# adaLN groups 3 to 5 on GpSimd instead of TensorE, in a two-layer diffusion backbone

## The chip, the cores and the metric

The kernel runs on one core of a Trainium2 chip. The metric is the device time of one execution in microseconds. TensorE multiplies matrices, VectorE (DVE in the profile) and ScalarE (ACT) do the elementwise work, GpSimd (POOL) takes some additions and a few transfers, and SyncE (SP) issues most of the loads.

## The reference, cut to what matters

The network has two layers over 512 latent and 256 context tokens of width 1024. Each layer is modulated by a vector `mod` of 6 x 1024 numbers, which comes from a product of the condition with `w_ada`, once for the latent tokens (`c`) and once for the context tokens (`c_ctx`):

```python
for l in range(DEPTH):
    mod   = silu_c  @ w_ada[l] + b_ada[l]        # w_ada: (2, 1024, 6144)
    mod_c = silu_cc @ w_ada[l] + b_ada[l]
    sh1, sc1, gt1, sh2, sc2, gt2 = jnp.split(mod, 6, axis=-1)
    h = modulate(rmsnorm(x, g_mix[l]), sh1, sc1)
    ...                                          # w_in, attention and convolution
    x = x + gt1 * merge_groups(...)
    h2 = modulate(rmsnorm(x, g_ffn[l]), sh2, sc2)
    x = x + gt2 * swiglu(h2, w_gate_up[l], w_down[l])
    ...                                          # the same for ctx, in layer 0 only
```

The result is the latent stream after a last RMSNorm. `mod` of layer 1 is needed only once layer 0 is over, so its product can be done at any time before.

## The kernel before, in words

Features lie on the partitions, 128 at a time, and tokens in the free dimension (768 in layer 0, 512 in layer 1). Each layer goes through phases in a fixed order, `PHASES`: `u`, `qkv`, attention, `ob`, `oa`, and then the feed-forward part in three chunks of 8, 8 and 6 tiles: `gu0`, `dn0`, `gu1`, `dn1`, `gu2`, `dn2`. A phase is a row of blocks of weights, two (a pair, `j` = 0 and 1) for each `i`: `gu0` and `gu1` have 16 blocks, `gu2` 12, each `dn` phase 8. One block of layer 0 is `tile_product` (L457): for each of 8 k-tiles (6 in `dn2`) three products (high x high, low x high, high x low) over two column ranges, so 48 (36) matmuls. `after` lets another piece of work be issued behind a certain k of a block.

The weights are split on the chip: SP loads `raw`, ScalarE copies it to `w_high` (`split_high`, L677), VectorE subtracts (`split_low`, L945, `w_low`). In a `gu` phase VectorE reads a product out of PSUM (`scale_product`, L989), then does `split_low` for the next pair, after the second product multiplies gate and value (L1283), and forms `ff_low` (L1287) once ScalarE has made `ff_high`. The next `dn` phase waits for one `ff_low` tile at each k of its first block (`ready`).

The adaLN product is cut into 6 groups, three for each layer, of 2048 columns, and each group into 8 units, one for each 128 rows of `w_ada`. A unit is a tile of 128 x 2048 numbers (1 MB). `ada_unit` (L406) multiplies it on TensorE with the 32 columns of `cond` (of which two are used), in four products of 512 columns that lie side by side in the array and add up in PSUM over the 8 units. Then ScalarE copies the sum (`ada_rows`), TensorE turns it (`ada_turn`) and VectorE adds the bias and forms the gains (`ada_columns`). Group 0 runs at the start, groups 1 and 2 in `u` and `qkv` of layer 0, and groups 3, 4 and 5, which are layer 1's, in `dn0`, `dn1` and `dn2` of layer 0: one unit after each block. Their tiles are loaded by SP between the loads of `raw`, into two places in turn. A phase with units is written out; the others are loops over `i`.

GpSimd has nothing to do from the end of `oa` of layer 0 up to layer 1's convolution. Each engine runs its own stream in order; semaphores tie them together. `Chain.link` makes an instruction of an engine wait for the one before it.

Of the kernel before, what the change touches and what calls it, by code (L numbers as in the profile page):

```python
# [27 lines left out]
P = 128  # L28
D = 1024
DT = D // P  # L30
# [23 lines left out]
AG = 3  # L54
# [70 lines left out]
def hybrid_backbone(nc, xT, params, w_ada, w_conv, w_mix, w_out, w_gu, w_dn0, w_dn1, w_dn2,  # L125
                    rope, ident_in, masks_in, out):
    with ExitStack() as ctx:
# [13 lines left out]
        ada_in_qkv = wD[:].rearrange("p j g m -> p (j g m)")  # L141
        ssum = sb("ssum", [P, T])
# [3 lines left out]
        ada_row = act_out[:, 0:AGW // 4]  # L146
# [4 lines left out]
        diag = scratch[:].rearrange("p (b t) -> p b t", t=P)  # L151
        par = sb("par", [P, COLS])
# [9 lines left out]
        ones = sb("ones", [P, P])  # L162
        per_tok = sb("per_tok", [P, 2, TB])
# [9 lines left out]
        with ExitStack() as h_scope:  # L173
# [22 lines left out]
            with ExitStack() as s:  # L196
                s.enter_context(nc.sbuf_tensor("gap_ff", [P, 2 * max(CHUNKS) * T], F32))
                ada_in_ff = s.enter_context(nc.sbuf_tensor("ada_in_ff", [P, AGW], F32))
            with ExitStack() as s:
# [26 lines left out]
        ada_in = [sem(f"ada_in{j}") for j in range(2)]  # L226
        first_in = [sem(f"ada_first_in{j}") for j in range(DT)]
# [7 lines left out]
        ada_mm, ada_rowed = sem("ada_unit_done"), sem("ada_rows_copied")  # L235
        ada_tr, ada_cols = sem("ada_rows_transposed"), sem("ada_columns_ready")
# [82 lines left out]
        def ada_units(layer, name, block):  # L319
# [4 lines left out]
            at = (0, 1, 1, 2, 3, 3, 4, 5) if name == "qkv" else [k * (blocks - 1) // (DT - 1) for k in range(DT)]  # L324
# [3 lines left out]
        ADA_PLACES, uses, last_use = {}, [0, 0], [DT, DT]  # L328
        for g in range(1, 2 * AG):
            for k in range(DT):  # L330
# [4 lines left out]
                ADA_PLACES[g, k] = (tile, ada_in[place], 16 * uses[place], last_use[place])  # L335
                last_use[place] = g * DT + k + 1
        for k in range(DT):
            ADA_PLACES[0, k] = (ada_first[k][:] if k < DT - 1 else ada_raw[:], first_in[k], 16, 0)
# [8 lines left out]
        def _(sp):  # L347
            sp.dma_start(par[:], params).then_inc(par_in, 16)

            def load_ada(unit):  # L350
                tile, landed, _, free = ADA_PLACES[unit]
                if free:
                    sp.wait_ge(ada_mm, free)
# [49 lines left out]
        def _(pe):  # L403
# [11 lines left out]

            def ada_turn(g):

                pe.wait_ge(ada_rowed, g + 1)
                for j in range(4):
                    last = nc.tensor.transpose(bank[:, SMALL, P * j:P * j + P], ada_row[:, P * j:P * j + P], ident[:])  # L420
# [78 lines left out]
            def phase(layer, name, ktiles, rhsH, rhsL, cols, ready=None, key=None, blocks=TB):  # L499
# [3 lines left out]
                after = {0: [], 1: []}  # L503
                if key is not None:
# [997 lines left out]
```

## Time and profile before

| | us |
|---|---|
| median of three runs | 1657.31 (1656.78 to 1658.14) |
| the profiled execution | 1658.43 |
| its span | 1656.1 |
| TensorE busy | 1570.3 (95%) |
| VectorE busy | 837.1 (51%) |
| ScalarE busy | 570.1 (34%) |
| GpSimd busy | 126.3 (8%) |

The span is the time from the first to the last instruction of the profiled execution. In the views, PE is TensorE's matmuls and PEld its weight loads. L465 is the product in `tile_product`, L412 the one in `ada_unit`, L420 the turn in `ada_turn`. A line like "x<-x,tmp" names the tile written and the tiles read.

### The profile page before, as it was taken

Reading aid. Unit: us, or ns where it says so; the run is one execution under the profiler, and the core shown is the slowest. Engines: PE = TensorE matmul, PEld = TensorE weight load, DVE = VectorE, ACT = ScalarE, POOL = GpSimd, SP = SyncE. Lnnn points to the kernel's source line nnn. Section 1 sums busy time; section 2 is a strip of 40 time slices with the busy share of each in tenths; the row PEclk is TensorE's granted clock in tenths of the full one; section 3 lists DMA queues with packets and bytes.
Section 4 is the critical chain, followed back from the end, with each engine's and each line's share of the span. In section 5 each row is a group of like instructions: output and inputs, shape, how many; then the busy total and the mean of one; then the engine's idle time right before and its main releaser. Section 6 shows DMA issues by size and latency. Waiting matters only on the chain.

```text
span 1656.1 us, 25043 instructions
## 1 busy us (share of the span) xinstructions
PE 1570.3 (95%) x9804; PEld 1278.1 (77%) x9804; DVE 837.1 (51%) x1527; ACT 570.1 (34%) x882; POOL 126.3 (8%) x162
## 2 busy tenths in 40 slices
PE   3899987999999999999999999988999999999997
PEld 0675654578888878888788878765578998998995
DVE  1484566867433322433233455767776443443445
ACT  2411258734443111221122233136845541321222
POOL 0032012021000000000000000521120000000000
PEclk9999988999999999999999999998999999999998
DMA  8474420002112442124412353511012223323222
GB/s 325 178 219 107 177 91 1 1 26 65 56 59 63 165 153 64 63 63 139 171 60 63 104 199 104 144 52 39 1 39 90 89 90 100 89 89 100 91 76 88
DMA packets 39865, 161.19 MB, mean 97 GB/s; under 512 B 5616, under 2 KB 6000, under 8 KB 33648
## 3 DMA queue, kind: packets, MB, share of 16 engines
q1 hardware_dynamic: 35856, 148.72, 26.7%
q0 software_dynamic: 3936, 11.45, 2.6%
q8 instruction: 51, 0.84, 0.2%
q14 instruction: 22, 0.18, 0.0%
HBM read 149.76 MB, written 2.10 MB: 92 GB/s over the span
## 4 chain that ended last, share of the span: by engine, by line
PE 84%; DVE 7%; ACT 4%; issue 2%; DMA 2%; SPq 1%; POOL 0%; DVEq 0%; ACTq 0%; POOLq 0%
PE banks L465 71%; PE banks L494 3%; PE banks L572 2%; PE banks L584 2%; PE banks L599 2%; PE banks L412 2%; DMA x<-in_xT 1%; PE banks L452 1%; PE banks L435 1%; DVE w_low L949 1%; ACT prob L765 1%; DVE ssum L956 1%; DMA raw<-in_w_mix 0%; ACT w_high L684 0%; DVE row_max L1048 0%
## 5 line engine op out<-in xcount | busy, mean ns | idle before, releaser
L465 PE MATMUL banks<-h_high,w_high 128*128 128x512 f32 (+1 forms) x1856 | 433.3, 315 | 5.0 <-DVE h_low L978 3.5
L465 PE MATMUL banks<-h_high,w_low 128*128 128x512 f32 (+1 forms) x1856 | 428.8, 313 | 0.0
L465 PE MATMUL banks<-h_low,w_high 128*128 128x512 f32 (+1 forms) x1856 | 428.6, 312 | 0.0
L684 ACT ACTIVATE w_high<-raw 128x1024 fp32r<-128x1024 f32 (+1 forms) x178 | 185.5, 1042 | 672.8 <-PE banks L465 664.5
L949 DVE TENSOR_TENSOR w_low<-raw,w_high 128x1024 fp32r<-128x1024 f32 (+1 forms) x178 | 217.6, 1222 | 238.7 <-ACT w_high L684 236.6
L465 PEld LDWEIGHTS banks<-h_high,w_high 128*128 128x128 f32 x1856 | 289.0, 190 | 40.1 <-issue 18.8
L465 PEld LDWEIGHTS banks<-h_low,w_high 128*128 128x128 f32 x1856 | 288.4, 190 | 21.6
L465 PEld LDWEIGHTS banks<-h_high,w_low 128*128 128x128 f32 x1856 | 287.3, 190 | 21.6
L992 DVE COPY shift_product<-banks 128x2 f32<-128x2 f32 x116 | 18.4, 159 | 354.0 <-PE banks L465 342.2
L465 PE MATMUL banks<-ff_high,w_high 128*128 128x512 f32 (+1 forms) x528 | 162.5, 362 | 0.5 <-DVE ff_low L1287 0.5
L465 PE MATMUL banks<-ff_low,w_high 128*128 128x512 f32 (+1 forms) x528 | 160.0, 357 | 0.0
L465 PE MATMUL banks<-ff_high,w_low 128*128 128x512 f32 (+1 forms) x528 | 160.0, 357 | 0.0
L465 PEld LDWEIGHTS banks<-ff_high,w_high 128*128 128x128 f32 x528 | 86.8, 188 | 33.3 <-issue 17.6
L465 PEld LDWEIGHTS banks<-ff_low,w_high 128*128 128x128 f32 x528 | 87.0, 188 | 15.9
L465 PEld LDWEIGHTS banks<-ff_high,w_low 128*128 128x128 f32 x528 | 86.9, 188 | 16.0
L993 DVE TENSOR_TENSOR tmp<-banks,inv_root 128x768 f32<-128x768 f32 (+1 forms) x116 | 95.1, 820 | 0.1
L572 PE MATMUL banks<-k_stacked,q_stacked 128*128 128x384 f32 (+2 forms) x224 | 63.3, 389 | 12.9 <-ACT esink L767 8.0
L1048 DVE TENSOR_REDUCE row_max<-banks 128x1 f32<-128x512 f32 (+2 forms) x80 | 55.2, 690 | 32.8 <-PE banks L572 32.6
L901 ACT ACTIVATE ff_high<-tmp 128x768 f32 (+3 forms) x44 | 32.5, 740 | 97.9 <-DVE tmp L1283 97.9
L1024 DVE SCALAR_TENSOR_TENSOR x<-banks,mod,x 128x512 f32 (+1 forms) x96 | 60.3, 656 | 11.1 <-PE banks L465 11.0
L1287 DVE TENSOR_TENSOR ff_low<-tmp,ff_high 128x768 f32 (+3 forms) x44 | 36.3, 826 | 43.7 <-ACT ff_high L901 43.7
L777 ACT ACTIVATE probT<-banks 128x512 f32<-128x512 f32 (+2 forms) x80 | 48.0, 600 | 29.2 <-PE banks L584 28.7
(147 smaller groups left out, 1582.9 us busy)
## 6 DMA issues: line engine op xcount, KB each, us to landing
raw<-in_w_gu SPq DMA_DIRECT2D x88, 512.0 KB, 3.5
ada_raw<-in_w_ada SPq DMA_DIRECT2D x21, 1024.0 KB, 5.1
raw<-in_w_dn SPq DMA_DIRECT2D x32, 512.0 KB, 3.6
raw<-in_w_mix SPq DMA_DIRECT2D x28, 512.0 KB, 5.5
ada_in_ff<-in_w_ada SPq DMA_DIRECT2D x12, 1024.0 KB, 5.0
raw<-in_w_out SPq DMA_DIRECT2D x16, 512.0 KB, 3.6
ada_first<-in_w_ada SPq DMA_DIRECT2D x7, 1024.0 KB, 13.5
raw<-in_w_dn SPq DMA_DIRECT2D x16, 384.0 KB, 3.0
```

The lines of the kernel that those rows point to most:

```text
L412: last = mm(bank[32 * q:32 * q + 32, ADA, :], cond[:, k, :], tile[:, 512 * q:512 * q + 512], start=(k == 0), stop=(k == DT - 1), tile_posi ...
L465: last = mm(bank[:, 2 * slot + bk, 0:b - a], weights[w][:, k0_w + k, :], rhs[:, k0_rhs + k, a:b], start=(k == 0 and n == 0), stop=(k == kt ...
L494: last = mm(bank[QC * q:QC * q + QC, BC + bk, 0:b - a], wD[:, j, g, QC * q:QC * q + QC], zr[j][:, q, SH * g + a:SH * g + b], start=(g == 0 ...
L572: last = mm(wide[:, at:at + w], lhs, rhs, start=in_bank[m] not in in_bank[:m], stop=in_bank[m] not in in_bank[m + 1:], skip_group_check=True)
L584: last = nc.tensor.transpose(wide[:, 512 * PTB + P * m:512 * PTB + P * m + P], probs[u % 4][:, P * m:P * m + P], ident[:])
L684: f(wH[j][:, 0:k, :], raw[j][:, 0:k, :], ACT.Copy).then_inc(w_high, 1)
L777: f(PT[:, group % 2, 0:w, i % 2 * 2 + i // 2, :], wide[:, 512 * PTB:512 * PTB + P * w].rearrange("p (k q) -> p k q", k=w), ACT.Copy).then_ ...
L949: tt(wL[j][:, 0:k, :], raw[j][:, 0:k, :], f32(wH[j][:, 0:k, :]), ALU.subtract).then_inc(w_low, 1)
L993: tt(like(tmp[slot]), src, like(rs), ALU.mult).then_inc(slot_free[slot], 1)
L1024: last = stt(out=xt, in0=bank[:, 2 * slot + (a >= N), 0:b - a], scalar=mod[:, layer, bass.ds(t + gate * DT, 1), v], in1=xt, op0=ALU.mult, ...
L1048: nc.vector.reduce_max(mx[:, c:c + 1], score_place(u, qs[q][2]), AX.X).then_inc(row_ok, 1)
L1287: tt(aL[:, i, 0:width], tmp[1][:, 0:width], f32(aH[:, i, 0:width]), ALU.subtract).then_inc(ff_low, 1)
```

## The change

Groups 3 to 5 leave `ada_unit`. GpSimd loads their 24 tiles itself, from two places in turn, as soon as its own work in `oa` of layer 0 is done. For each tile and for each of the two conditions (v = 0, 1) it multiplies with the column of `cond` of that tile, each partition by its own number, and adds the product to a running sum `ada_sums[v]` of 128 x 2048, in two halves of 1024 columns. The running sums lie in `w_conv` and where `ssum`, `sq` and `tmp` begin to be laid out in a scope of their own. After the eighth tile of a group TensorE adds the partitions once (`ada_sum`): `pick` has a column of ones at place v, so eight products give the two rows. `ada_sum` and the turn stand in the second block of `gu1` for group 3, in the second block of `gu2` for group 4 and in the last block of `gu2` for group 5, behind k = 1 and k = 6. The first tile of a group waits until TensorE has read the group before. `gu1`, `gu2` and the `dn` phases of layer 0 change their form with it: the `dn` phases become loops, and the last pair of `gu2` is written out.

```diff
+        ada_sums = [ada_in_qkv, ada_sum_ctx[:]]
+        ada_row = [act_out[:, 0:AGW // 4]] * 3 + [scratch[:, 0:AGW // 4]] * 3
...
-        ADA_IN = {(0, "u"): 1, (0, "qkv"): 2, (0, "dn0"): 3, (0, "dn1"): 4, (0, "dn2"): 5}
-
-        TURN_IN = {(0, "qkv"): 1, (0, "gu1"): 3, (0, "gu2"): 4, (1, "u"): 5}
+        ADA_IN = {(0, "u"): 1, (0, "qkv"): 2}
+        SUM_IN, TURN_IN = {(0, "gu1"): 3, (0, "gu2"): 4}, {(0, "qkv"): 1}
+        LAST_SUM = (0, "gu2")
...
+            def ada_sum(g):
+
+                pe.wait_ge(ada_read, DT * (g - 2))
+                for v in range(2):
+                    for q in range(4):
+                        last = mm(bank[32 * q:32 * q + 32, ADA, :], pick[:, v, :], ada_sums[v][:, 512 * q:512 * q + 512],
+                                  start=(v == 0), stop=(v == 1), tile_position=(0, 32 * q))
+                last.then_inc(ada_mm, 1)
...
+                if (layer, name) in SUM_IN:
+                    g = SUM_IN[layer, name]
+                    after[1].append((1, lambda: ada_sum(g)))
+                    after[1].append((DT - 2, lambda: ada_turn(g)))
...
                 if loop:
-                    with pe.Fori(1, pairs) as i:
+                    with_sum = (layer, name) == LAST_SUM
+                    with pe.Fori(1, pairs - with_sum) as i:
                         for j in range(2):
                             gemm_block(layer, name, i, j, ktiles, rhsH, rhsL, cols)
+                    if with_sum:
+                        for j in range(2):
+                            gemm_block(layer, name, pairs - 1, j, ktiles, rhsH, rhsL, cols,
+                                       after=[(1, lambda: ada_sum(5)), (DT - 2, lambda: ada_turn(5))] if j else ())
...
+                if layer == 0:
+                    later = [(g, k) for g in range(3, 2 * AG) for k in range(DT)]
+
+                    def load_ada(unit):
+                        tile, landed, _, free = ADA_PLACES[unit]
+                        pool.wait_ge(*free)
+                        pool.dma_start(tile, w_ada[unit[0], unit[1]]).then_inc(landed, 16)
+
+                    pool.wait_ge(gemm, 2 * USES[layer, "gu0"])
+                    for unit in later[0:2]:
+                        load_ada(unit)
+                    pool.wait_ge(diag_ok, root_index[layer, "n2"] + 1)
+                    for at, unit in enumerate(later):
+                        tile, landed, count, _ = ADA_PLACES[unit]
+                        pool.wait_ge(landed, count)
+                        if unit[1] == 0:
+                            pool.wait_ge(ada_mm, 3 * DT + unit[0] - 3)
+                        for h in range(2):
+                            half = slice(h * AGW // 2, (h + 1) * AGW // 2)
+                            for v in range(2):
+                                c = cond[:, unit[1], v:v + 1]
+                                if unit[1] == 0:
+                                    last = nc.gpsimd.tensor_scalar(ada_sums[v][:, half], tile[:, half], c, None, ALU.mult)
+                                else:
+                                    chain.link(nc.gpsimd.tensor_scalar(ada_part[:], tile[:, half], c, None, ALU.mult))
+                                    last = nc.gpsimd.tensor_tensor(ada_sums[v][:, half], ada_sums[v][:, half], ada_part[:],
+                                                                   ALU.add)
+                                if h + v < 2:
+                                    chain.link(last)
+                        last.then_inc(ada_read, 1)
+                        pool.wait_ge(ada_read, at + 1)
+                        if at + 2 < len(later):
+                            load_ada(later[at + 2])
```

Left out of the diff: ScalarE's and VectorE's `ada_rows` and `ada_columns` move with the sums (the first and last tile of `gu1` and `gu2`), and the waits are renumbered.

## Rows read from the trace of the kernel before

**Rows 1.** The page: its first line, and the chain that ended last by engine.
```profile
span 1656.1 us, 25043 instructions
...
PE 84%; DVE 7%; ACT 4%; issue 2%; DMA 2%; SPq 1%; POOL 0%; DVEq 0%; ACTq 0%; POOLq 0%
```

**Rows 2.** Chain in order of time, `dn0` to `dn2`: start us, us, what.
```profile
560.60 1.00 PE banks L412 x8
...
627.94 0.99 PE banks L412 x8
...
845.97 0.44 PE banks L420 x4
846.40 103.49 PE banks L465 x588
949.89 0.99 PE banks L412 x8
...
994.93 1.00 PE banks L412 x8
```

**Rows 3.** GpSimd's groups, shapes apart: xcount | busy us, mean ns | idle before.
```profile
L1382 POOL TENSOR_TENSOR ssum<-ssum,conv 128x768 f32<-128x768 f32 x1 | 1.8, 1849 | 0.1
...
L1341 POOL DMA_DIRECT2D w_conv<-in_w_conv x6 | 3.5, 592 | 0.3 <-issue 0.3
...
L1382 POOL TENSOR_TENSOR ssum<-ssum,conv 128x512 f32<-128x512 f32 x1 | 1.3, 1291 | 0.1
...
L1335 POOL MEMSET cond<- 128x256 f32 x1 | 0.3, 312 | 0.3 <-POOLq L1494 0.3
L1337 POOL MEMSET ones<- 128x128 f32 x1 | 0.2, 205 | 0.0
```

**Rows 4.** GpSimd in order of time: start us, us, engine, line, operation.
```profile
153.79 1.86 POOL L1380 TENSOR_TENSOR ssum<-conv 128x768 f32<-128x768 f32 x1
155.72 1.85 POOL L1382 TENSOR_TENSOR ssum<-ssum,conv 128x768 f32<-128x768 f32 x1
...
353.39 2.80 POOL L1409 TENSOR_TENSOR x<-x,tmp 128x768 f32<-128x768 f32 x1 [1.51 <-DVE tmp L1035]
```

**Rows 5.** VectorE in order of time, beside those GpSimd instructions.
```profile
244.75 0.15 DVE L1061 TENSOR_TENSOR psums<-psums,esink 128x1 f32<-128x1 f32 x1
...
246.90 1.80 DVE L1061 TENSOR_TENSOR psums<-psums,esink 128x1 f32<-128x1 f32 x1
...
353.26 1.23 DVE L949 TENSOR_TENSOR w_low<-raw,w_high 128x1024 fp32r<-128x1024 f32 x1
```

**Rows 6.** GpSimd in order of time, layer 0's attention.
```profile
244.88 7.59 POOL L1404 TENSOR_TENSOR z_padded<-z_padded,inv_root 128x768 f32<-128x768 f32 x4 [32.90 <-ACT inv_root L705]
```

**Rows 7.** VectorE's groups in 841 to 944 us (`gu2` of layer 0), shapes apart.
```profile
L949 DVE TENSOR_TENSOR w_low<-raw,w_high 128x1024 fp32r<-128x1024 f32 x11 | 13.5, 1226 | 8.5 <-ACT w_high L684 8.2
...
L1287 DVE TENSOR_TENSOR ff_low<-tmp,ff_high 128x768 f32 x5 | 4.8, 959 | 5.7 <-ACT ff_high L901 5.7
L1283 DVE SCALAR_TENSOR_TENSOR tmp<-tmp,shift_product,act_out 128x512 f32<-128x512 f32 x5 | 3.7, 746 | 0.0
L1283 DVE SCALAR_TENSOR_TENSOR tmp<-tmp,shift_product,act_out 128x256 f32<-128x256 f32 x5 | 2.4, 480 | 0.0
```

**Rows 8.** VectorE in order of time, the `n2` diagonals of layer 0.
```profile
422.49 1.27 DVE L971 TENSOR_SCALAR diagonals<-ident,per_tok 128x128 f32<-128x128 f32 x6
```

**Rows 9.** Chain in order of time, the first blocks of the kernel.
```profile
52.54 11.04 PE banks L465 x48
...
64.58 8.65 PE banks L465 x48
```

**Rows 10.** TensorE in order of time, the first products of `dn0`.
```profile
551.96 0.51 PE L465 MATMUL banks<-ff_high,w_high 128*128 128x512 f32 x2
```

**Rows 11.** VectorE in order of time, the last tile of `gu0`.
```profile
552.16 0.16 DVE L992 COPY shift_product<-banks 128x2 f32<-128x2 f32 x1 [6.12 <-PE banks L465]
...
556.46 0.96 DVE L1287 TENSOR_TENSOR ff_low<-tmp,ff_high 128x768 fp32r<-128x768 f32 x1 [0.91 <-ACT ff_high L901]
```

**Rows 12.** TensorE's waits over the whole kernel: us in total, times, longest.
```profile
PE banks L465 <- DVE ff_low L1287: 0.5, 1, 0.5
```

More of the change, by code:

```diff
@@ L226, in hybrid_backbone @@
         ada_in = [sem(f"ada_in{j}") for j in range(2)]
+        ada_late_in = [sem(f"ada_late_in{j}") for j in range(2)]
         first_in = [sem(f"ada_first_in{j}") for j in range(DT)]
@@ L323, in ada_units @@
             blocks = 2 * PAIRS_OF[name]
-            at = (0, 1, 1, 2, 3, 3, 4, 5) if name == "qkv" else [k * (blocks - 1) // (DT - 1) for k in range(DT)]
+            at = (0, 1, 1, 2, 3, 3, 4, 5) if name == "qkv" else [blocks // DT * k for k in range(DT)]
             return [(ADA_IN[layer, name], k) for k in range(DT) if at[k] == block]
-        ADA_PLACES, uses, last_use = {}, [0, 0], [DT, DT]
+        ADA_PLACES, uses, last_use = {}, [0, 0], [(ada_mm, DT), (ada_mm, DT)]
         for g in range(1, 2 * AG):
@@ L352, in load_ada @@
                 if free:
-                    sp.wait_ge(ada_mm, free)
+                    sp.wait_ge(*free)
                 if unit == (ADA_IN[0, "qkv"], 1):
@@ L513, in phase @@
                                    after[j] if i == 0 else ())
-                        for u in ada_units(layer, name, 2 * i + j):
-                            ada_unit(u)
+                        if with_ada:
+                            for u in ada_units(layer, name, 2 * i + j):
+                                ada_unit(u)
                         if (name, 2 * i + j) in CONV_AFTER:
@@ L627, in attention @@
                     values(len(qs) - 1, m)
-            pe.wait_ge(consts, 4)
+            pe.wait_ge(consts, 5)
             pe.wait_ge(cond_ok, 1)
@@ L891, in _, with gu_pair @@
                     ff = layer * FT + sum(CHUNKS[:c])
-                    def gu_pair(i):
+                    def gu_pair(i, first=False, last=False):
                         split_high(layer, gu, i, 0)
@@ L896, in gu_pair @@
                         for a, b, v in streams(context):
-                            last = f(act_out[:, a:b], tmp[0][:, a:b], ACT.Silu, bias=shifted[:, 0, v:v + 1])
-                        last.then_inc(gate_ok, 1)
+                            gate = f(act_out[:, a:b], tmp[0][:, a:b], ACT.Silu, bias=shifted[:, 0, v:v + 1])
+                        gate.then_inc(gate_ok, 1)
+                        if last and (layer, gu) == LAST_SUM:
+                            ada_rows(5)
+                        if first and (layer, gu) in SUM_IN:
+                            ada_rows(SUM_IN[layer, gu])
                         split_high(layer, gu, i, 1)
@@ L901, in gu_pair @@
                         f(aH[:, i, 0:width], tmp[1][:, 0:width], ACT.Copy).then_inc(ff_high, 1)
-                    with act.Fori(0, tiles - 1) as i:
+                    gu_pair(0, first=True)
+                    with act.Fori(1, tiles - 1) as i:
                         gu_pair(i)
-                    gu_pair(tiles - 1)
+                    gu_pair(tiles - 1, last=True)
                     def dn_pair(i, more=True):
@@ L1189, in _ @@
                         taps(10 * i - 5, 10 * i + (i == 3))
-                    if layer and i == 0:
-                        ada_columns(ADA_IN[0, "dn2"])
                 for i in range(3):
@@ L1288, in gu_pair @@
                         dve.wait_ge(ff_low, i + (ff + 1))
-                    with dve.Fori(0, tiles - 1) as i:
+                    gu_pair(0)
+                    if (layer, gu) in SUM_IN:
+                        ada_columns(SUM_IN[layer, gu])
+                    with dve.Fori(1, tiles - 1) as i:
                         gu_pair(i)
                     gu_pair(tiles - 1)
+                    if (layer, gu) == LAST_SUM:
+                        ada_columns(5)
                     def dn_pair(i, more=True):
@@ L1337, in _ @@
             nc.gpsimd.memset(ones[:], 1.0).then_inc(consts, 1)
+            nc.gpsimd.memset(pick[:], 0.0).then_inc(consts, 1)
+            pool.wait_ge(consts, 4)
+            for v in range(2):
+                nc.gpsimd.memset(pick[:, v, v:v + 1], 1.0)
             nc.gpsimd.memset(mean_col[:, 0:1], 1.0 / D)
@@ L1369, in _ @@
                 if layer:
-                    pool.wait_ge(ada_mm, DT * (ADA_IN[0, "qkv"] + 1))
+                    pool.wait_ge(ada_mm, 3 * DT + 3)
                 for k in (1, 2):
```

28 lines of the change are left out of this document (17 added, 11 removed).

## The prediction

> **What bounds the kernel now.** I read the page first. The profiled execution took 1658.43 us, with a span of 1656.1 us; the median of the three timed runs is 1657.31. 84% of the chain that ended last is TensorE [rows 1]. So whatever leaves TensorE's stream in layer 0 comes off the time, and whatever makes TensorE wait is added. Then I read the chain in order of time through the feed-forward part of layer 0. The reader is to see there that the adaLN units stand on the chain itself, one behind each block of `dn0`, `dn1` and `dn2` [rows 2]. All changes below are made against the profiled execution and carried over to the median.
>
> **What is removed.** The chain has 103.49 us for 588 products, which is 12.25 blocks of 48, so 8.45 us for a block with nothing between its products [rows 2]. In `dn0` the units stand at 560.60 and, seven later, at 627.94: a period of 9.62 us, so one unit costs 1.17 us (0.99 of its own and some 0.2 where TensorE changes over). In `dn2` a block has 36 products, 6.34 us at the same rate; the period is (994.93 - 949.89) / 6 = 7.51 us, again 1.17 [rows 2]. 24 units leave: 24 x 1.17 = **28.1 us off**. Their 24 loads leave SP's queue for GpSimd's. SP has no wait for them on the chain, so that is worth nothing.
>
> **What is added to TensorE.** `ada_sum` issues eight such products, two rounds of the four that make a unit: 2 x 0.99 + 0.2 = 2.2 us, three times: **6.6 us on**. The three turns are as many as before at 0.44 us each [rows 2] and only move. ScalarE copies the rows of the sum while TensorE does k = 2 to 6 of the same block, 5 x 1.06 = 5.3 us, so the turn finds them ready. The new columns work on VectorE is a few instructions of 16 columns. The unrolled `dn` phases become loops like `gu2`, whose blocks are those of 8.45 us, so the form costs nothing. Balance so far: -28.1 + 6.6 = -21.5 us.
>
> **What GpSimd has to do for one group.** The sums of a group take, for k = 0, four one-input instructions of 128 x 1024, and for k = 1 to 7 four pairs of one multiplication and one addition: 32 multiplications and 28 additions, each waiting for the one before by `chain.link`.
> - Addition (two inputs): 1849 ns for 768 columns and 1291 ns for 512 [rows 3], so 2.18 ns a column and 2407 ns for 1024. From one linked instruction to the next is 155.72 - 153.79 = 1.93 us against 1.86 us of the instruction [rows 4], so 0.07 us more each. 28 x 2.48 = 69.4 us.
> - Multiplication by a column (one input): no row shows one on GpSimd. From below it is bounded by the memset, which reads nothing: 312 ns for 256 columns, 205 ns for 128 [rows 3], 0.84 ns a column, so 0.95 us for 1024. From above by the addition, which reads twice: 2.41 us. I take 1.2 us, near the memset, since one stream of input is missing there and the addition's second stream is missing too. 32 x 1.27 = 40.6 us.
> - Issue of the loads: 6 fall inside the time of the last group, and 592 ns is what such an issue takes for half the size [rows 3]: 6 x 0.59 = 3.5 us, at most 7.
> So W = 113 us for a group if nobody is in the way; 152 with the upper bound, 105 with the lower.
>
> On the multiplication the Trainium skill speaks too (GPSIMD Engine Reference, "Engine selection"): a one-input operation on GpSimd runs at roughly line rate, a two-input one at about half VectorE's speed. By that the multiplication would be some 1.0 us, an estimate from that page, and the sum below some 6 us smaller. No trace here shows it.
>
> **GpSimd and VectorE get in each other's way.** An addition of GpSimd that began at 353.39 took 2.80 us instead of 1.85; VectorE's `w_low`, with two SBUF inputs, had begun at 353.26 and ran its usual 1.23 us [rows 4, 5]. The other way round, while GpSimd does four additions in a row from 244.88 [rows 6], an addition of one column on VectorE that should take 0.15 us takes 1.80 us and ends with the GpSimd instruction [rows 5]. So the two exclude each other for the length of an instruction, in order of arrival.
> VectorE's instructions with two SBUF inputs in a stretch of ten `gu2` blocks: 10 `w_low` at 1.23, 5 pairs of L1283 at 0.75 + 0.48, 5 of L1287 at 0.96 [rows 7]: 23.3 us. In the one case where I can see it, 0.95 of 1.23 us came on top of GpSimd's instruction, so I count D = 21 us; its bounds are 0 (they slip between) and 23.
>
> **Where the groups must be done.** Group 3 starts when the `n2` diagonals are made, at 422.49 + 1.3 = 423.8 [rows 8], and is wanted in the second block of `gu1`. That is some 210 us later: `gu0` and `dn0` are 24 blocks. Even 152 + 33 (VectorE in `gu0`) + 12 fits. Group 4 starts when the sum of 3 is read and is wanted 24 blocks later, 203 us: it fits also. Group 5 can't start before TensorE has read group 4 in `gu2`'s second block, since the running sums are the same two tiles, and it is wanted in `gu2`'s twelfth block after k = 1. Between them lie k = 2 to 7 of block 1, nine blocks, and k = 0 and 1 of block 11: ten blocks and a turn, 84.5 + 0.4 = **84.9 us**. GpSimd needs W + D = 113 + 21 = 134 us. TensorE stands at `pe.wait_ge(ada_read, 24)` for 134 - 85 = **49 us**; behind that wait are the rest of the block and all of `dn2`, so nothing hides it. Bounds: 105 - 85 = 20 us; 152 + 23 + 3 - 85 = 93 us.
> After such a rest TensorE starts slowly: the first 48 products after its early wait took 11.04 us against 8.65 for the next [rows 9]: **2.4 us**.
>
> **The two turns from `gu` to `dn`.** The first block of `dn0` wants `ff_low` of the last tile at its k = 7, 551.96 + 7.4 = 559.4 [rows 10]. VectorE begins the tail at 552.16 and ends `ff_low` at 557.42 [rows 11]: 1.9 us to spare. The tail has four instructions that can meet GpSimd. `w_low` comes at a random moment (about 1 us of wait), the two of L1283 come right behind another, with a GpSimd instruction let in between (half 2.48, half 1.27: 1.9 us each), and `ff_low` comes 0.9 us later (about 0.9): 5.5 us, so 3.6 us late. GpSimd is still at work then in `gu0` (95 of its 113 us are done by 552) and `gu1`: 2 x 3.6 = **7 us**; bounds 0 and 2 x (4 x 2.48 - 1.9) = 16. At `gu2` the whole group is done before `dn2` starts; the 0.5 us that TensorE waits for `ff_low` in the whole kernel stay [rows 12]. In the middle of a phase the same delays are hidden: a pair's `w_low` is wanted 8.45 us or more after its product is read.
>
> **The sum.** -28.1 + 6.6 + 49 + 2.4 + 7 = +36.9 us. Profiled execution 1658.4 + 37 = 1695, median 1657.3 + 37 = **1694 us**.
>
> **The rivals.**
> 1. *The multiplication costs as much as the addition.* W = 152, the wait 152 + 21 - 85 = 88 us: 1657.3 - 21.5 + 88 + 2.4 + 7 = 1733. For it: GpSimd's two-input rate is itself far from one column a cycle, so its programs may be slow whatever they read. Against: the memset row. 17%.
> 2. *GpSimd and VectorE hardly meet.* D = 0 and no late `ff_low`: wait 28 us, 1657.3 - 21.5 + 28 + 2.4 = 1666. For it: only short overlaps are seen. Against: both directions are in the trace. 12%.
> 3. *Faster: at 1024 columns GpSimd works at the memset's rate in the additions too*, 0.95 us each. Place: group 5 in `gu2`. Then W = 60 x 1.02 + 3.5 = 65 us and 65 + 19 fits into 85; nothing is left but the balance: 1657.3 - 21.5 = 1636. It decides from W + D under 85 + 12 = 97 us, 12 us for a unit; there the wait is smaller than what is saved net of the late `ff_low` and the slow start. Against: the slope of 2.18 ns a column between 512 and 768. 8%.
> Between rivals 2 and 3 lies a narrow case of no difference: 3%.
>
> **How the numbers follow.** Forecast 60% (own range 1680 to 1712: the multiplication at 0.95 to 1.5 us, the late `ff_low` at 0 to 11 us), rival 1 17%, rival 2 12%, rival 3 8%, no difference 3%. The range is to leave out rival 3 and the case of no difference and takes in the bounds of the wait, 20 to 93 us: 1657.3 - 21.5 + 20 + 2.4 = 1658 to 1657.3 - 21.5 + 93 + 2.4 + 11 = 1742; I put the low end at 1661. About 0.2%, 3.3 us, is what a measurement of this kernel tells from no change. Faster 0.08, same 0.04, slower 0.88.
>
> **What would show it.** In the changed kernel's profile: `dn` blocks of layer 0 at 8.45 and 6.34 us without units; GpSimd multiplications of 128 x 1024 near 1.2 us and additions near 2.4, some longer by a VectorE instruction; groups 3 and 4 done before they are wanted; one long TensorE wait for GpSimd in the last block of `gu2`, some 49 us, with ScalarE and VectorE idle in it; short waits for `ff_low` early in `dn0` and `dn1`. The prediction is wrong if a unit takes GpSimd less than 12 us, if the wait stands elsewhere (at `gu1` or `gu2`'s start), or if TensorE waits for `w_low` within the phases.

## The result, and the profile after

The changed kernel takes 1727.26 us (median of four runs, 1725.49 to 1728.79) against 1657.72 us for the kernel before beside it: a ratio of 1.042, 95% interval 1.0402 to 1.0438. It is slower by 69.5 us. The forecast was 1694 us within 1661 to 1742; the measured time lies inside these bounds, near their upper end, and outside the forecast's own narrower range of 1680 to 1712.

First the changed kernel's page: the span, the busy time of the engines, the chain that ended last by engine and the start of its list by line.

```profile
span 1724.2 us, 24982 instructions
...
PE 1548.5 (90%) x9660; PEld 1275.2 (74%) x9660; DVE 910.3 (53%) x1527; ACT 535.9 (31%) x856; POOL 646.2 (37%) x369
...
PE 75%; POOL 10%; DVE 7%; ACT 4%; issue 2%; DMA 1%; SPq 1%; DVEq 0%; ACTq 0%; POOLq 0%
```

TensorE did less work (1548.5 us busy, 1570.3 before) and the kernel is longer all the same; GpSimd, which had no share of the chain [rows 1], has 10% of it. TensorE's waits over the whole kernel say where (us in total, times, longest):

```profile
PE banks L434 <- POOL ada_sum_context L1476: 91.2, 1, 91.2
...
PE banks L487 <- DVE w_low L985: 0.7, 1, 0.7
PE banks L487 <- DVE ff_low L1321: 0.5, 1, 0.5
```

In the changed kernel's rows L434 is the product in `ada_sum`, L487 the one in `tile_product` and L442 the turn. The new loss is one wait, at `ada_sum(5)`. The waits for `w_low` and `ff_low` stay under 1 us each; the one for `ff_low` is as long as before [rows 12]. The chain in order of time shows the rest of the layer (start us, us, what). These lines answer to [rows 2].

```profile
424.60 204.03 PE banks L487 x1158
628.63 1.85 PE banks L434 x16
630.48 5.46 PE banks L487 x30
635.95 0.44 PE banks L442 x4
636.38 197.73 PE banks L487 x1122
834.12 1.90 PE banks L434 x16
836.06 0.13 issue
836.19 2.85 POOL w_conv L1473
...
1009.87 2.35 POOL ada_sum_context L1476
1012.26 3.64 PE banks L434 x16
1015.90 6.48 PE banks L487 x30
1022.38 0.44 PE banks L442 x4
1022.82 51.95 PE banks L487 x294
```

The reader sees `gu0` and `dn0` in one unbroken piece of products (1158 in 204.03 us, so 8.46 us for 48), a sum of 1.85 us where eight units were, and the same for `gu1` and `dn1`. From 836.19 us the chain is GpSimd's, until the third sum at 1012.26. The forecast named this place. What it missed is why the piece is so long. GpSimd's groups, shapes apart, in 420 to 1100 us (xcount | busy us, mean ns | idle before); they answer to [rows 3]:

```profile
L1475 POOL TENSOR_SCALAR ada_part<-ada_in_ff,cond 128x1024 f32<-128x1024 f32 x48 | 151.2, 3151 | 4.1
L1475 POOL TENSOR_SCALAR ada_part<-ada_raw,cond 128x1024 f32<-128x1024 f32 x36 | 111.1, 3087 | 3.1
L1476 POOL TENSOR_TENSOR ada_sum_context<-ada_sum_context,ada_part 128x1024 f32<-128x1024 f32 x42 | 106.1, 2525 | 3.5
L1476 POOL TENSOR_TENSOR w_conv<-w_conv,ada_part 128x1024 f32<-128x1024 f32 x42 | 102.7, 2444 | 3.5
```

The multiplication, which reads one tile, takes longer than the addition, which reads two. In the chain, where TensorE waits and VectorE is idle, a unit is quite regular (start us, us, what):

```profile
946.86 2.86 POOL ada_part L1475
949.79 2.35 POOL w_conv L1476
952.14 0.09 issue
952.22 2.85 POOL ada_part L1475
...
968.26 0.51 issue
968.76 0.60 POOL ada_in_ff L1457
969.41 2.86 POOL ada_part L1475
```

A pair of a multiplication and an addition takes 952.22 - 946.86 = 5.36 us, a unit (all that GpSimd does with one tile) 969.41 - 946.86 = 22.55 us: four pairs and 1.1 us for its last semaphore and the issue of the next load.

After the wait TensorE is slow for a moment. The columns are the stretch, its length, the busy us of PE, PEld, DVE, ACT and POOL, the granted clock, the DMA share and GB/s; the granted clock goes from 1.00 (2.4 GHz) down to 0.53 in the wait (nearly all of it at 1.2 GHz), and is 0.75 in the mean just after:

```profile
836.00:921.00 85.00, 85.00 (x484) 74.21 (x484) 47.73 (x48) 20.50 (x26) 80.84 (x31) 1.00 0.28 95
921.00:1012.00 91.00, 0.07 (x1) 0.00 (x0) 0.00 (x0) 0.18 (x1) 86.59 (x36) 0.53 0.11 39
1012.00:1024.00 12.00, 11.74 (x58) 7.78 (x59) 0.08 (x1) 0.68 (x2) 0.21 (x1) 0.75 0.01 1
```

The third sum took 3.64 us instead of 1.85, and the 30 products behind it 6.48 instead of 5.46: 2.8 us in all.

The sum of what is seen: 23 units at 1.17 us off (-26.9; why 23 and not 24 is told below), three sums at 1.87 (+5.6), the wait (+91.2), the slow start (+2.8): +72.7 us. The chain can be measured over the same stretch in both kernels, from the start of the first long piece of products to the last product of `dn2`. In the kernel before this stretch began and ended so:

```profile
426.50 134.09 PE banks L465 x762
...
995.92 6.57 PE banks L465 x36
```

It took 1002.49 - 426.50 = 575.99 us, and in the changed kernel 1074.77 - 424.60 = 650.17: +74.2 us. Beyond the 72.7 that is the third turn (0.44 us), which stood in layer 1 before, and 1.1 us spread over the products. The spans differ by 68.1 us only: 1.9 us were gained before the stretch (424.60 instead of 426.50) and 4.2 behind it. Of the latter, 1.6 us are in the first pieces of layer 1, where the granted clock was 0.73 before (1009.3 to 1022 us) and 0.86 after (1081.6 to 1094 us), and 0.4 the turn; the rest isn't traced. The kernel before itself varies from 1651.4 to 1658.3 us over the runs below, so differences of this size outside the stretch aren't put down to the change.

### The profile page after: what moved, and what is told of

It is laid out like the page before. It is cut to its first block, busy times and chain, and to the rows that moved or that the text cites. A ratio compares the mean times of both kernels' runs of the same rounds, so it can differ in the third digit from the quotient of the medians.

```text
span 1724.2 us, 24982 instructions
## 1 busy us (share of the span) xinstructions
PE 1548.5 (90%) x9660; PEld 1275.2 (74%) x9660; DVE 910.3 (53%) x1527; ACT 535.9 (31%) x856; POOL 646.2 (37%) x369
## 3 DMA queue, kind: packets, MB, share of 16 engines
q1 hardware_dynamic: 32400, 123.56, 21.5%
## 4 chain that ended last, share of the span: by engine, by line
PE 75%; POOL 10%; DVE 7%; ACT 4%; issue 2%; DMA 1%; SPq 1%; DVEq 0%; ACTq 0%; POOLq 0%
PE banks L487 63%; POOL ada_part L1475 5%; PE banks L516 3%; PE banks L604 2%; PE banks L616 2%; POOL ada_sum_context L1476 2%; POOL w_conv L1476 2%; PE banks L631 2%; DMA x<-in_xT 1%; PE banks L474 1%; PE banks L457 1%; DVE w_low L985 1%; ACT prob L797 1%; PE banks L425 1%; DVE ssum L992 0%
## 5 line engine op out<-in xcount | busy, mean ns | idle before, releaser
L487 PE MATMUL banks<-h_high,w_high 128*128 128x512 f32 (+1 forms) x1856 | 433.8, 315 | 4.1 <-DVE h_low L1014 3.5
L487 PE MATMUL banks<-h_high,w_low 128*128 128x512 f32 (+1 forms) x1856 | 429.2, 313 | 0.0
L487 PE MATMUL banks<-h_low,w_high 128*128 128x512 f32 (+1 forms) x1856 | 428.7, 312 | 0.0
L985 DVE TENSOR_TENSOR w_low<-raw,w_high 128x1024 fp32r<-128x1024 f32 (+1 forms) x178 | 249.3, 1401 | 181.1 <-ACT w_high L716 178.8
L487 PEld LDWEIGHTS banks<-h_high,w_high 128*128 128x128 f32 x1856 | 289.5, 190 | 39.8 <-issue 18.4
L487 PEld LDWEIGHTS banks<-h_low,w_high 128*128 128x128 f32 x1856 | 288.7, 190 | 21.6
L487 PEld LDWEIGHTS banks<-h_high,w_low 128*128 128x128 f32 x1856 | 287.3, 190 | 21.6
L487 PE MATMUL banks<-ff_high,w_high 128*128 128x512 f32 (+1 forms) x528 | 160.5, 358 | 0.5 <-DVE ff_low L1321 0.5
L487 PE MATMUL banks<-ff_high,w_low 128*128 128x512 f32 (+1 forms) x528 | 160.5, 358 | 0.0
L487 PE MATMUL banks<-ff_low,w_high 128*128 128x512 f32 (+1 forms) x528 | 160.4, 358 | 0.0
L1475 POOL TENSOR_SCALAR ada_part<-ada_in_ff,cond 128x1024 f32<-128x1024 f32 x48 | 151.2, 3151 | 4.1
L1475 POOL TENSOR_SCALAR ada_part<-ada_raw,cond 128x1024 f32<-128x1024 f32 x36 | 111.1, 3087 | 3.1
L1476 POOL TENSOR_TENSOR ada_sum_context<-ada_sum_context,ada_part 128x1024 f32<-128x1024 f32 x42 | 106.1, 2525 | 3.5
L1476 POOL TENSOR_TENSOR w_conv<-w_conv,ada_part 128x1024 f32<-128x1024 f32 x42 | 102.7, 2444 | 3.5
L487 PEld LDWEIGHTS banks<-ff_high,w_high 128*128 128x128 f32 x528 | 87.1, 188 | 17.0 <-DVE ff_low L1321 0.9
L487 PEld LDWEIGHTS banks<-ff_high,w_low 128*128 128x128 f32 x528 | 87.1, 188 | 16.1
L487 PEld LDWEIGHTS banks<-ff_low,w_high 128*128 128x128 f32 x528 | 87.1, 188 | 16.0
L1398 POOL DMA_DIRECT2D z_shifted<-z_padded x96 | 46.9, 497 | 128.4 <-issue 81.3
L434 PE MATMUL banks<-w_conv,pick_stream 128*32 128x512 f32 x24 | 4.1, 757 | 91.2 <-POOL ada_sum_context L1476 91.2
```

The source lines that it names most:

```text
L487: last = mm(bank[:, 2 * slot + bk, 0:b - a], weights[w][:, k0_w + k, :], rhs[:, k0_rhs + k, a:b], start=(k == 0 and n == 0), stop=(k == kt ...
L985: tt(wL[j][:, 0:k, :], raw[j][:, 0:k, :], f32(wH[j][:, 0:k, :]), ALU.subtract).then_inc(w_low, 1)
L1398: pool.dma_start(zr[k % 2][QC * c:QC * c + QC, q, 0:w], z[QC * q:QC * q + QC, k, c:c + w])\
L1475: chain.link(nc.gpsimd.tensor_scalar(ada_part[:], tile[:, half], c, None, ALU.mult))
L1476: last = nc.gpsimd.tensor_tensor(ada_sums[v][:, half], ada_sums[v][:, half], ada_part[:], ALU.add)
```

## The experiments

**Only the first tile of each group has arithmetic.** This separates the wait from everything else that the change does. All 24 tiles are still loaded.

```diff
+                        if unit[1] == 0:
...
-                                    chain.link(nc.gpsimd.tensor_scalar(ada_part[:], tile[:, half], c, None, ALU.mult))
-                                    last = nc.gpsimd.tensor_tensor(ada_sums[v][:, half], ada_sums[v][:, half], ada_part[:],
-                                                                   ALU.add)
...
+                        else:
+                            last = nc.gpsimd.tensor_copy(ada_part[:, 0:1], tile[:, 0:1])
```

> The changed kernel, but GpSimd does its arithmetic for the first tile of each group only (the other seven tiles are loaded and not added, so layer 1's modulation is left incomplete). Theory A: the added time is TensorE's single wait of 91.2 us for group 5 and the slow start behind it (about 2.9 us); everything else of the change is a gain. Then this is 1727.3 - 91.2 - 2.9 = 1633 us, no wait of TensorE for GpSimd, and w_low back at 1.23 us. Worked out from the edit, 23 units at 1.17 off and three sums at 1.9 on give 1657.7 - 26.9 + 5.6 = 1636. Theory B (GpSimd's work costs TensorE time in the phases too, by making VectorE late): clearly below 1633, say 1625.

Measured: 1634.60 us (1634.27 to 1635.99) against 1655.13 for the kernel before; ratio 0.9876 (0.9853 to 0.9899). TensorE waits nowhere for GpSimd's sums, so their loads alone delay nothing. Theory A said 1633; B's 1625 isn't met. Better than the total is the chain: `gu0` and `dn0` took the same time with idle GpSimd as in the changed kernel, where GpSimd was at work all the while (there 204.03 and 197.73 us as well).

```profile
424.69 204.03 PE banks L487 x1158
...
636.48 197.73 PE banks L487 x1122
```

So GpSimd's work beside VectorE, as the changed kernel has it, costs TensorE nothing in these phases, to a hundredth of a microsecond. The gain of taking the units away, 20.5 us here in the medians and 19.8 in the chain from the first long piece to the last product of `dn2` (556.18 us against 575.99), is close to the 21.5 of the forecast's balance.

**Additions only.** Without the multiplications of tiles 1 to 7, the time of a group is tested term by term.

```diff
-                                    chain.link(nc.gpsimd.tensor_scalar(ada_part[:], tile[:, half], c, None, ALU.mult))
-                                    last = nc.gpsimd.tensor_tensor(ada_sums[v][:, half], ada_sums[v][:, half], ada_part[:],
+                                    last = nc.gpsimd.tensor_tensor(ada_sums[v][:, half], ada_sums[v][:, half], tile[:, half],
```

> The changed kernel without the multiplications of tiles 1 to 7: GpSimd adds the tile itself to both running sums (the factor is left out of the computation). Theory A (a group's time is the sum of its instructions, and the multiplication at 2.93 us from start to start was the term that was too small): a group takes 7 x 11.1 + 12.8 - 1 = 89 us and 7 to 12 us for VectorE's turns, so TensorE waits 11 to 16 us for group 5: about 1633 + 14 + 2 = 1649, about equal to or a little faster than the kernel before. Theory B (VectorE's two-input instructions are shut out and counted in full, 21 us): the wait is 25 us, 1660. Theory C (something other than the arithmetic delays group 5, such as the loads): the wait stays above 60 us.

Measured: 1651.63 us (1650.45 to 1654.19); ratio 0.9977 (0.9966 to 0.9988), just faster than the kernel before. TensorE's wait for group 5 (its waits over the whole kernel):

```profile
PE banks L434 <- POOL ada_sum_context L1475: 12.8, 1, 12.8
```

12.8 us lie inside Theory A's 11 to 16, not at the 25 of B or above the 60 of C (the loads). The multiplications are worth 91.2 - 12.8 = 78.4 us of the wait: 28 x 2.93 = 82 less some of VectorE's turns, which now all fall on additions.

**Multiplication by a fixed number.** Is it the column of the condition that makes it slow?

```diff
-                                    chain.link(nc.gpsimd.tensor_scalar(ada_part[:], tile[:, half], c, None, ALU.mult))
+                                    chain.link(nc.gpsimd.tensor_scalar(ada_part[:], tile[:, half], 0.5, None, ALU.mult))
```

> The changed kernel with the multiplication of tiles 1 to 7 by the number 0.5 instead of a column with one number for each partition (the condition is left out there). If the column makes the multiplication slow, it falls from 2.85 us to 1.0 to 1.5 us, group 5 takes some 40 us less and TensorE's wait falls from 91 to about 50 us: 1685. If it is the operation's own rate, it stays at 2.85 us and the time at 1727.

Measured: 1727.39 us in one run, the wait 88.0 us. The multiplication took nearly as long with VectorE at work beside it (3007 and 3053 ns in the mean, 3151 and 3087 in the changed kernel), and 2.77 instead of 2.85 us while VectorE is idle:

```profile
953.11 2.77 POOL L1475 TENSOR_SCALAR ada_part<-ada_in_ff 128x1024 f32<-128x1024 f32 x1
```

The column is worth 0.08 us of the 2.85; it is not the cause. The time didn't fall with the wait because TensorE waited 2.3 us in three pieces for `ff_low` here, where it waited 0.5 in the changed kernel.

**The multiplication as a two-input instruction.** The same result, with the column read again for each element.

```diff
-                                    chain.link(nc.gpsimd.tensor_scalar(ada_part[:], tile[:, half], c, None, ALU.mult))
+                                    chain.link(nc.gpsimd.tensor_tensor(ada_part[:], tile[:, half],
+                                                                       c.to_broadcast([P, AGW // 2]), ALU.mult))
```

> The changed kernel, same result, but the multiplication is a two-input instruction: tile times the condition's column read again for each of the 1024 columns (step zero). If GpSimd's cost goes with the kind of instruction, the multiplication falls from 2.85 us to the addition's 2.40, a group takes 28 x 0.45 = 13 us less, and TensorE's wait is 91 - 13 = 78 us, a few more if VectorE is shut out longer: about 1716. If it goes with the arithmetic (multiplying by a column), 2.85 stays and the time is 1727.

Measured: 1712.67 us in one run, the wait 67.9 us, more saved than I expected. GpSimd in order of time, while TensorE waits:

```profile
945.25 1.90 POOL L1475 TENSOR_TENSOR ada_part<-ada_in_ff,cond 128x1024 f32<-128x1024 f32 x1
947.23 2.34 POOL L1477 TENSOR_TENSOR w_conv<-w_conv,ada_part 128x1024 f32<-128x1024 f32 x1
```

The two-input form takes 1.90 us, below the addition and a third below the one-input form. So the same multiplication costs less as a two-input instruction than as a one-input one, the opposite order of the one that I had assumed. Why it is also cheaper than the addition (2.34 us) no run isolates. Multiplying as such isn't the reason: with two full inputs, four multiplications of 768 columns took 7.59 us in the kernel before [rows 6], 1.9 us each, like the additions of that size [rows 3]. What is left is the second input, one column read with a step of zero. The two-input form has a price of its own: TensorE now waits 7.0 us, in three pieces of up to 3.4, for `ff_low`:

```profile
PE banks L487 <- DVE ff_low L1321: 7.0, 3, 3.4
```

The two long pieces of products, with the turns from `gu` to `dn` in them, take 208.85 and 202.94 us instead of 204.03 and 197.73, 10.0 us more together. That is why the time falls by 14.6 us and not by the 23.3 us of the wait. This is the late `ff_low` that the forecast had expected for the changed kernel.

**One-input instructions only.** How long does each kind keep VectorE out?

```diff
-                                    last = nc.gpsimd.tensor_tensor(ada_sums[v][:, half], ada_sums[v][:, half], ada_part[:],
-                                                                   ALU.add)
+                                    last = nc.gpsimd.tensor_scalar(ada_sums[v][:, half], ada_part[:], c, None, ALU.mult)
```

> The changed kernel with each addition replaced by a second multiplication of one input (so the sum over the tiles is left out; the running sums hold only the last tile). Theory A: a one-input instruction of GpSimd keeps VectorE's two-input instructions out only for a part of its 2.85 us (some 0.9 us, while it reads), a two-input one for its whole 2.4 us. Then w_low in gu0 to dn1 falls from a mean of 1.76 us to 1.2 to 1.45 and ff_low from 2.1 to under 1.4, although GpSimd is busier. Theory B: any GpSimd instruction keeps VectorE out for its full length: w_low at 1.8 us or more. In both the group takes 28 x 0.45 = 13 us more, so the wait is about 100 us and the time 1737.

Measured: 1739.65 us in one run, the wait 101.7 us, as expected in both theories. GpSimd and then VectorE in order of time, one stretch of `gu0`:

```profile
450.88 2.85 POOL L1476 TENSOR_SCALAR w_conv<-ada_part,cond 128x1024 f32<-128x1024 f32 x1
...
466.85 2.85 POOL L1475 TENSOR_SCALAR ada_part<-ada_raw,cond 128x1024 f32<-128x1024 f32 x1
```

```profile
451.13 1.95 DVE L985 TENSOR_TENSOR w_low<-raw,w_high 128x1024 fp32r<-128x1024 f32 x1
...
468.02 1.22 DVE L985 TENSOR_TENSOR w_low<-raw,w_high 128x1024 fp32r<-128x1024 f32 x1
469.17 1.14 DVE L1317 SCALAR_TENSOR_TENSOR tmp<-tmp,shift_product,act_out 128x512 f32<-128x512 f32 x2
```

A `w_low` that comes 1.17 us after a multiplication's start (468.02 against 466.85) runs at its usual 1.22 us, inside it. One that comes 0.25 us after a start (451.13 against 450.88) takes 1.95 us, so it began in earnest some 1.0 us after that start. In the changed kernel a `ff_low` meets an addition:

```profile
864.91 2.40 POOL w_conv L1476
```

```profile
865.16 2.96 DVE L1321 TENSOR_TENSOR ff_low<-tmp,ff_high 128x768 f32 x1 [1.14 <-ACT ff_high L937]
```

It ends at 868.12, 0.81 us after the addition's end at 867.31. Its usual time is 0.96 us, so it ran only when the addition was all but over. The means over `gu0` to `dn1`, in ns, from VectorE's groups of each kernel:

| | before | changed | additions only | one input only |
|---|---|---|---|---|
| `w_low`, 1024 columns | 1226 | 1762 | 1582 | 1316 |
| L1283 / L1317, 512 columns | 746 | 1516 | 2138 | 1058 |
| L1283 / L1317, 256 columns | 480 | 661 | 1545 | 584 |
| `ff_low` (the larger group) | 959 | 2145 | 1936 | 1261 |

The columns aren't equally full of GpSimd's work: it was busy 349 of these 412 us in the changed kernel and 188 with additions only, where it had its groups done early, so that column is diluted. With one input only the means fall into the bounds of Theory A (1.2 to 1.45 us for `w_low`, under 1.4 for `ff_low`). Theory A holds: the one-input multiplication keeps VectorE's two-input instructions out for about its first microsecond only, the addition to its end. The Trainium skill ("SBUF — State Buffer", section "SBUF: two separate sides") says that whichever of the two starts first holds the shared port pair for the whole instruction. For GpSimd's additions the trace agrees (the 2.96 us above); for its multiplications it doesn't (1.0 of 2.85 us).

**Pieces of 512 columns.** What of each instruction goes with the columns?

```diff
-                        for h in range(2):
-                            half = slice(h * AGW // 2, (h + 1) * AGW // 2)
+                        for h in range(4):
+                            half = slice(h * AGW // 4, (h + 1) * AGW // 4)
...
```

> The changed kernel with every multiplication and addition in two pieces of 512 columns, same result: it gives what of each instruction goes with the columns. The addition should take 1.29 us, as the 512-column addition of the kernel before. The multiplication: 1.5 us if its 2.85 us are all per column, 2.0 us or more if a large part is fixed. With 1.5 the group takes 60 x 0.25 = 15 us more and the time is 1742; with 2.0 it takes 32 us more, 1760.

Measured: 1763.20 us in one run. GpSimd in order of time, while TensorE waits:

```profile
962.59 1.56 POOL L1475 TENSOR_SCALAR ada_part<-ada_raw,cond 128x512 f32<-128x512 f32 x1
964.24 1.26 POOL L1476 TENSOR_TENSOR ada_sum_context<-ada_sum_context,ada_part 128x512 f32<-128x512 f32 x1
```

The multiplication goes from 2.85 to 1.56 us, so 2.5 ns a column and 0.27 us fixed; the addition from 2.35 to 1.26, 2.1 ns a column and 0.17 fixed. Most of the multiplication is a rate, as the lower of my two cases had it. The time is above that case's 1742 all the same, so the time was forecast wrong. The two multiplications and two additions that now stand for a pair take 2 x 3.01 = 6.02 us instead of 5.36; the 0.66 us, where I had reckoned with 0.5, make the wait for group 5 20 us longer (111.4). Groups 3 and 4 were late too: TensorE waited three times, 118.9 us in all. These are 27.7 of the 35.9 us by which this run is above the changed kernel. Another 2.6 are in the first two sums (2.70 and 3.69 us instead of 1.85 and 1.90, each behind a wait); the rest isn't traced.

**Only groups 3 and 4 on GpSimd.** If the deadline of group 5 is the whole loss, leaving it on TensorE keeps the gain. The edit, in its main lines:

```diff
-        ADA_IN = {(0, "u"): 1, (0, "qkv"): 2}
+        ADA_IN = {(0, "u"): 1, (0, "qkv"): 2, (0, "dn2"): 5}
...
-                    later = [(g, k) for g in range(3, 2 * AG) for k in range(DT)]
+                    later = [(g, k) for g in range(3, 5) for k in range(DT)]
```

> Only groups 3 and 4 on GpSimd, group 5 on TensorE in dn2 as before. Theory A: groups 3 and 4 are ready long before they are wanted (GpSimd needs some 175 us for a group and has 203 to 210), so TensorE never waits for GpSimd, and 16 units at 1.17 less two sums at 1.9 are won: 1657.7 - 15 = 1643. Theory B (GpSimd beside VectorE also delays TensorE within gu and dn): 1650 or more, with waits for w_low or ff_low in the trace.

Measured: 1638.99 us (1638.75 to 1640.29); ratio 0.9902 (0.9879 to 0.9925). Theory A expected 15 us under the kernel before, and it is 16.1 against the 1655.13 beside it (the expected 1643 was reckoned from 1657.7); in the chain from the first long piece to the last product of `dn2` it is 14.2 (561.77 us against 575.99). TensorE never waits for GpSimd's sums, and `gu0` with `dn0` again takes 204.03 us. This version is faster than both kernels, and 1.0% faster than the one before.

**Group 5 shared.** The 85 us of `gu2` that GpSimd has for group 5 can be used for a part of it, with TensorE adding its own units to the same sum in PSUM. I timed three versions beside each other: none, three and four tiles of group 5 on GpSimd, the last with the two-input multiplication in group 5. The edit for four tiles, in its main lines, against the version with none:

```diff
-                    later = [(g, k) for g in range(3, 5) for k in range(DT)]
+                    later = [(g, k) for g in range(3, 5) for k in range(DT)] + [(5, k) for k in range(4)]
...
-                                  start=(v == 0), stop=(v == 1), tile_position=(0, 32 * q))
+                                  start=(v == 0), stop=(v == 1 and g < 5), tile_position=(0, 32 * q))
```

> The kernel with groups 3 and 4 on GpSimd and group 5 on TensorE, timed again beside the two that share group 5, on the same chip: 15 to 18 us under the kernel before, so 1639 to 1642, with GpSimd never waited for in gu and dn.

> As the kernel with group 5 shared, but GpSimd does three tiles of it with the one-input multiplication of the change: 12.8 + 2 x 25 = 63 us, 20 us of room. Three units (3.5 us) leave, a sum (1.9 us) comes: 1.6 us less than with group 5 wholly on TensorE, 1637.5. No wait of TensorE for GpSimd or for ff_low beyond 0.5 us. If it is not below the kernel with group 5 on TensorE, a sum costs as much as three units.

> Groups 3 and 4 on GpSimd as in the change; of group 5 GpSimd does the first four tiles within gu2 (with the multiplication as a two-input instruction, 1.89 us) and TensorE the last four in dn2, into the same sum. Theory: GpSimd needs 4 x 2.93 + 3 x 4 x (1.97 + 2.42) + 4 = 68 us and some 10 for VectorE's turns, under the 84.9 us between group 4's sum and group 5's, so TensorE doesn't wait; against the kernel with group 5 wholly on TensorE four units (4.7 us) leave and a sum (1.9 us) comes: 2.8 us less, 1636. Rival: GpSimd's two-input instructions make VectorE's ff_low late at dn2 or the four tiles are late; then a wait of TensorE of 3 us or more takes it back, 1639 or above.

Measured, against 1657.14 us (1651.35 to 1658.13) for the kernel before:

| tiles of group 5 on GpSimd | median us | range | ratio to before |
|---|---|---|---|
| none | 1639.57 | 1636.13 to 1639.84 | 0.9897 (0.9879 to 0.9915) |
| three | 1637.35 | 1636.36 to 1638.89 | 0.9888 (0.9871 to 0.9905) |
| four | 1635.47 | 1634.71 to 1636.49 | 0.9876 (0.9857 to 0.9896) |

None of the three waits for GpSimd's sums; the waits for `ff_low` stay at 0.5 us in each. The steps of 2.2 and 4.1 us are of the size expected (1.6 and 2.8), but the ranges and the intervals overlap, so the medians alone show only an order that agrees with the theory. The chains show the size: from the start of the first long piece of products to the last product of `dn2` they take 561.76, 560.36 and 559.17 us, so three tiles win 1.4 us and four 2.6. The version with four tiles has the lowest median of all, 21.7 us under the kernel before. Its chain goes through `gu2` without a gap at the third sum (start us, us, what; L437 is the product in `ada_sum` here, L490 the one in `tile_product`, L445 the turn):

```profile
835.67 1.85 PE banks L437 x16
837.52 5.46 PE banks L490 x30
842.99 0.44 PE banks L445 x4
843.42 79.20 PE banks L490 x450
922.62 1.85 PE banks L437 x16
```

## Why the prediction was right in its place and too small in its size

The place of the loss and its mechanism were forecast; its size wasn't. A wait of 49 us was forecast and 91.2 measured, 42 us more, while everything else together came out some 10 us below its forecast (the late `ff_low`, which stayed away, is 7 of them). That the time still fell inside the wide range is luck in part, as the points on the multiplication and on VectorE's turns show.

- **The bound.** Right: everything is decided on TensorE's stream, and the loss is one wait of it.
- **The units removed.** 28.1 us were forecast. At 1.17 us a unit this stands, but the eighth unit of `dn2` was not on the path: it ran from 1002.41 us, while the chain goes from 1002.51 through ScalarE and VectorE to layer 1's first products at 1009.34, and only seven of that group stand in the chain of [rows 2]. 23 x 1.17 = 26.9.
- **The sums.** 2.2 us each were forecast, 1.85 and 1.90 measured, and the 30 products behind each take 5.46 us where 5.28 would be the rate of [rows 2]: 2.0 us. The balance of -21.5 came out at 19.8 us off in the chain of the first experiment and 20.5 in its medians.
- **Where the groups must be done.** Right. Group 5 had 84.9 us forecast; its first multiplication began at 836.19 and TensorE's wait at 1012.26 - 91.19 = 921.07, which is 84.9. Groups 3 and 4 were in time.
- **The multiplication.** This is the step that failed. I took 1.2 us, between 0.95 and 2.41; it is 2.85 us and lies above the upper bound. That bound rested on the thought that an instruction which reads one tile can't take longer than one which reads two, and no row showed that. With 2.93 instead of 1.27 us from start to start, 32 of them are 53 us more. Had I had the right value, the same sum would have given 49 + 53 = 102 us of wait, and 1747 in all. That would have been above the range's end of 1742. The Trainium skill (GPSIMD Engine Reference, "Engine selection") calls a one-input operation on GpSimd roughly line-rate, from which the prediction's estimate was 1.0 us. For this multiplication the runs don't bear that out: 2.85 us, and 2.77 with a fixed number.
- **The addition.** 2.41 us forecast from two shapes, 2.35 measured.
- **Between the units.** 0.59 us forecast, 1.1 measured: besides the issue of a load there is 0.5 us in which GpSimd waits for its own semaphore. Six times 0.5 is some 3 us in group 5.
- **VectorE's turns.** D = 21 us were forecast. Already by its own row it should have been less: 0.95 of 1.23 us is 77% and gives 18 of the 23.3 us. Four pairs an undisturbed unit, 22.55 us, seven times less the two loads that the last tiles don't issue, and the first tile with 13.0 give 168.6 us; group 5 took 1012.26 - 836.19 = 176.1, so D is 7.5 us. A one-input multiplication lets VectorE's instructions in after its first microsecond, and one that runs inside the rest costs GpSimd nothing (the multiplication at 466.85 above stays at 2.85 us). Only eleven of group 5's instructions were longer than undisturbed, by 0.2 to 1.1 us. This took back 13 of the 53 us, and 49 + 53 - 1 + 3 - 13 = 91 is the measured 91.2. Two errors of opposite sign stand in the forecast's wait. With the first alone put right the forecast would have been 1747, above the range; that the measured time lies inside it is luck, owed to this second error and to the next point.
- **`ff_low` late at the turns to `dn`.** 7 us forecast, 0 measured in the changed kernel. The working adds up to 1 + 1.9 + 1.9 + 0.9 = 5.7 us and not 5.5, which changes little. The idea isn't wrong: with two-input instructions alone on GpSimd's side the waits for `ff_low` are there, 7.0 us, and cost 10.0 us of the chain. But in the changed kernel `ff_low` of `gu0`'s last tile came 1.3 us later after its product than before (6.5 us after the start of VectorE's first read of it, 5.3 before), inside the 1.9 us to spare. How the instructions happen to meet counts too: with the multiplication 0.08 us shorter (the fixed number) the waits were 2.3 us.
- **The slow start.** 2.4 us forecast, 2.8 measured.
- **The rivals.** The first, a multiplication as dear as an addition, 1733 us, is the nearest to what came, and its doubt was right: an instruction of GpSimd can be slow though it reads one input. It had 17%; for the reason above it should have had more, since what spoke against it was a memset, which reads nothing. The second (engines hardly meet, 1666 us) is half true: they meet, with little effect while half of GpSimd's instructions read one input, but its time rested on the same price of the multiplication. The third fell with the additions at 2.35 us.

## What to carry to other kernels

Work moved to an idle engine has to be weighed against its deadline, not against that engine's idle share: two of the three groups were free and the third, with 85 us for 176 us of work, cost over four times what all three had won (94 us with the slow start, against 21). Give such an engine only what fits between the moment when its buffer comes free and the moment when its result is wanted, and leave the rest where it was; here that made a loss of 4.2% a gain of 1.2%. And where an instruction's price isn't in the trace, don't bound it by a similar instruction from above: measure one first.

## What the runs showed of the hardware

On GpSimd a one-input multiplication of 128 x 1024 fp32 numbers takes 2.85 us (2.5 ns a column and 0.27 us fixed, from the times at 512 and 1024 columns) with a column as factor, and 2.77 us with a fixed number. A two-input addition takes 2.35 us (2.1 ns a column and 0.17 us), and a two-input multiplication with the column spread by a step of zero takes 1.90 us. The one-input form keeps VectorE's instructions with two SBUF inputs out for some 1.0 us from its start (a `w_low` of 1.95 us), the two-input addition until it ends (a `ff_low` of 2.96 us). TensorE's granted clock was 0.53 over the 91 us without work, so nearly all of them at 1.2 GHz, the lower of its two levels (the other is 2.4 GHz), and 0.75 in the mean of the 12 us after.
